# Unread products in TensorE's waits, 128-column sums of squares, and differential attention with waits by head

## The reference, cut to what matters

```python
def rmsnorm(x, g):
    y = xf * lax.rsqrt(jnp.mean(xf * xf, axis=-1, keepdims=True) + EPS)
    return (y * g.astype(jnp.float32)).astype(x.dtype)

def attend(args):                      # differential attention, a block of 128 queries
    s = jnp.einsum('bqhcd,bkhcd->bhcqk', qblk, k).astype(jnp.float32)
    s = jnp.where(mask, s, -jnp.inf)   # causal
    p = jax.nn.softmax(s, axis=-1)
    a = p[:, :, 0] - lam * p[:, :, 1]  # two maps of 64 features per head
    return jnp.einsum('bhqk,bkhe->bqhe', a.astype(v.dtype), v)
```

## Time and profile before

| | us |
|---|---|
| median of 3 runs | 3038.07 (3037.4 to 3038.97) |
| the profiled execution | 3037.71 |
| its span | 3035.9 |
| mean granted clock of TensorE | 0.951 |
| TensorE busy | 2861.8 (94%) |
| its weight loads busy | 2733.2 (90%) |
| VectorE busy | 2017.9 (66%) |
| ScalarE busy | 1543.9 (51%) |
| GpSimd busy | 593.4 (20%) |

### The profile page before, as it was taken

The page is one execution under the profiler, slowest core; times in us unless marked ns, Lnnn a source line. Parts: engine busy times, 40 slices in busy tenths (PEclk is TensorE's granted clock), DMA queues, the critical chain, the costliest instruction groups (busy, mean ns, idle before and its releaser), DMA issues.

```text
span 3035.9 us, 61036 instructions
## 1 busy us (share of the span) xinstructions
PE 2861.8 (94%) x21416; PEld 2733.2 (90%) x21416; DVE 2017.9 (66%) x4423; ACT 1543.9 (51%) x3351; POOL 593.4 (20%) x648
## 2 busy tenths in 40 slices
PE   8898989999999999899889999999998999999998
PEld 7688879999999987788889999999987899986998
DVE  6759877677677655559777666666666755555555
ACT  8452344555555544552345555555555655554554
POOL 4522680011000013114660000000033410012100
PEclk9899999999999989699999999999998989898899
DMA  4035417676676543045327655555544045441454
GB/s 153 21 120 168 123 36 227 207 233 226 204 231 217 186 135 120 27 144 178 96 70 222 188 182 185 181 186 181 186 141 125 24 143 182 152 146 35 140 182 136
DMA packets 140810, 458.19 MB, mean 151 GB/s; under 512 B 15792, under 2 KB 33584, under 8 KB 140656
## 3 DMA queue, kind: packets, MB, share of 16 engines
q1 hardware_dynamic: 135120, 436.75, 45.7%
q0 software_dynamic: 5536, 19.47, 2.2%
HBM read 446.65 MB, written 9.50 MB: 150 GB/s over the span
## 4 chain that ended last, share of the span: by engine, by line
PE 87%; DVE 5%; ACT 4%; POOL 2%; issue 1%; DMA 0%; DVEq 0%; POOLq 0%; ACTq 0%; SPq 0%
PE banks L792 64%; PE banks L949 7%; PE banks L972 3%; PE banks L1071 2%; PE banks L813 2%; POOL x_lo L2439 2%; PE banks L869 1%; ACT w_hi L503 1%; ACT arena L1422 1%; PE banks L1204 1%; PE banks L1173 1%; PE banks L1260 1%; PE banks L823 1%; DVE onehot L2031 1%; PE banks L1240 1%
## 5 line engine op out<-in xcount | busy, mean ns | idle before, releaser
L510 DVE TENSOR_TENSOR w_lo<-ring,w_hi 128x512 fp32r<-128x512 f32 x1464 | 1019.7, 703 | 723.5 <-ACT w_hi L503 716.6
L503 ACT ACTIVATE w_hi<-ring 128x512 fp32r<-128x512 f32 x1464 | 916.3, 631 | 902.1 <-PE banks L792 856.6
L792 PE MATMUL banks<-x_hi,w_hi 128*128 128x256 f32 (+1 forms) x3072 | 885.9, 288 | 36.6 <-POOL x_lo L2439 21.8
L792 PE MATMUL banks<-x_lo,w_hi 128*128 128x256 f32 (+1 forms) x3072 | 876.3, 285 | 0.0
L792 PE MATMUL banks<-x_hi,w_lo 128*128 128x256 f32 (+1 forms) x3072 | 874.0, 285 | 0.0
L792 PE MATMUL banks<-gated_hi,w_hi 128*128 128x256 f32 x2560 | 727.8, 284 | 10.0 <-DVE gated_lo L2090 9.8
L792 PE MATMUL banks<-gated_hi,w_lo 128*128 128x256 f32 x2560 | 727.3, 284 | 0.0
L792 PE MATMUL banks<-gated_lo,w_hi 128*128 128x256 f32 x2560 | 726.0, 284 | 0.0
L792 PEld LDWEIGHTS banks<-x_hi,w_hi 128*128 128x128 f32 x3072 | 588.1, 191 | 47.8 <-issue 29.3
L792 PEld LDWEIGHTS banks<-x_lo,w_hi 128*128 128x128 f32 x3072 | 588.9, 192 | 0.6
L792 PEld LDWEIGHTS banks<-x_hi,w_lo 128*128 128x128 f32 x3072 | 589.0, 192 | 0.0
(11 more groups left out here) (333 smaller groups left out, 2905.2 us busy)
## 6 DMA issues: line engine op xcount, KB each, us to landing
ring<-in_peer_v SPq DMA_DIRECT2D x256, 512.0 KB, 3.5
ring<-in_peer_u SPq DMA_DIRECT2D x192, 512.0 KB, 3.5
arena<-in_peer_u SPq DMA_DIRECT2D x64, 512.0 KB, 3.6
ring<-in_mlp_up SPq DMA_DIRECT2D x64, 512.0 KB, 3.5
ring<-in_mlp_down SPq DMA_DIRECT2D x64, 512.0 KB, 3.5
ring<-w_peer_query SPq DMA_DIRECT2D x32, 512.0 KB, 3.5
ring<-w_fox_proj SPq DMA_DIRECT2D x24, 512.0 KB, 3.5
ring<-w_nsa_proj SPq DMA_DIRECT2D x20, 512.0 KB, 3.5
```

What stands on the lines that cost most here:

```text
L503: act.activation(w_hi[:, hn % SPLITS], raw_half(hn), ACT.Copy).then_inc(hi_ready, 1)
L510: dve.tensor_tensor(w_lo[:, hn % SPLITS], raw_half(hn), w_hi[:, hn % SPLITS].bitcast(F32), ALU.subtract)\
L792: mm = pe.matmul(out, w_at(w), x, start=start and j == 0, stop=stop and j == 2, skip_group_check=True)
```

## The change

A helper `keep_warm(n)` on TensorE makes n matmuls of 128 x 128 weights and 256 columns from `gated_hi` into bank 7, and nothing reads the results. GpSimd zeroes `gated_hi` at the start, and TensorE waits for that (`gated_cleared`). The helper stands at the load (40), ahead of the waits for squares (9), for the root (6) and behind the spread (14), ahead of the differential attention (20) and behind its first three scores (6 each). `sum_chunk` takes all 128 columns of `mean_w` (whose columns are alike) and `root_of` reads the first of each 128. In the differential attention TensorE waits for the remainders head by head, ScalarE stores a unit's turned map ahead of the exponentials, and one copy takes all of its keys, since the rest of 16 keys now lies right behind the others. Also in the kernel and left as they are: `norm_twice`'s products of two columns, and all stages that aren't named here.

```diff
--- before.py
+++ after.py
@@ -88,6 +88,8 @@
 EARLY_FIRST, EARLY_BESIDE = 20, 12
 EARLY = (EARLY_FIRST + EARLY_BESIDE,) * 2
 GROUPS_OF_TWO = SEQ // 2
+WARM_LOAD, WARM_SQUARES, WARM_ROOT, WARM_SCALE = 40, 9, 6, 14
+WARM_DIFF, WARM_FILL = 20, 6
 EXPS_BEFORE = {8: 0, 16: 1}
 SECOND_FINISH, SECOND_TURN = 48, 52
 
@@ -404,7 +406,7 @@
         presum_ready, h_final, h_final_pool = sem("presum_ready"), sem("h_final"), sem("h_final_pool")
         mo_ready, mo_scaled, v_kept = sem("mo_ready"), sem("mo_scaled"), sem("v_kept")
         x_landed = [sem(f"x_landed{j}") for j in range(NC // 2)]
-        taps_landed = sem("taps_landed")
+        taps_landed, gated_cleared = sem("taps_landed"), sem("gated_cleared")
         diagonal_ready, conv_summed = sem("diagonal_ready"), sem("conv_summed")
         subkeys_landed = sem("subkeys_landed")
         early_landed = [sem(f"early_landed{j}") for j in range(4)]
@@ -807,15 +809,22 @@
                                    x_hi[:, cc_, tk_], x_lo[:, cc_, tk_], cc_ == 0, cc_ == NC - 1)
                     mm.then_inc(half_used, 1)
 
+            def keep_warm(n):
+
+                for _ in range(n):
+                    pe.matmul(banks[:, 7, 0:SEQ], gated_hi[:, 0, 0:P], gated_hi[:, 0, :], start=True, stop=True)
+
             def sum_chunk(c, tokens, start, stop):
 
                 for i, (t0, m) in enumerate(norm_tiles(tokens)):
-                    mm = pe.matmul(banks[0:m, 4, i:i + 1], squares[:, c, t0:t0 + m], mean_w[:, 0:1], start=start and i == 0,
+                    mm = pe.matmul(banks[0:m, 4, i * P:(i + 1) * P], squares[:, c, t0:t0 + m], mean_w, start=start and i == 0,
                                    stop=stop, skip_group_check=True)
                 return mm
 
             def spread_rstd(n, tokens, src=None, at=0):
 
+                if src is None:
+                    keep_warm(WARM_ROOT)
                 pe.wait_ge(rstd_ready, n)
                 src = rstd_col if src is None else src
                 for i, (t0, m) in enumerate(norm_tiles(tokens)):
@@ -826,26 +835,31 @@
 
             def sum_squares(s, tokens):
 
+                keep_warm(WARM_SQUARES)
                 for c in range(NC):
                     pe.wait_ge(squares_ready, s["sq0"] + c + 1)
                     mm = sum_chunk(c, tokens, c == 0, c == NC - 1)
                 mm.then_inc(sum_ready, 1)
                 spread_rstd(s["su0"] + 1, tokens).then_inc(rstd_spread, 1)
+                keep_warm(WARM_SCALE)
 
             def sum_presummed(s, tokens):
 
+                keep_warm(WARM_SQUARES)
                 pe.wait_ge(presum_ready, s["ps0"] + 1)
                 for c in (0, NC - 2, NC - 1):
                     pe.wait_ge(squares_ready, s["sq0"] + c + 1)
                     mm = sum_chunk(c, tokens, c == 0, c == NC - 1)
                 mm.then_inc(sum_ready, 1)
                 spread_rstd(s["su0"] + 1, tokens).then_inc(rstd_spread, 1)
+                keep_warm(WARM_SCALE)
 
             def norm(s):
                 if s.get("squares"):
                     sum_squares(s, s["tokens"])
 
             def norm_twice(s):
+                keep_warm(WARM_SQUARES)
                 for c in range(NC):
                     pe.wait_ge(squares_ready, s["sq0"] + c + 1)
                     for i, (t0, m) in enumerate(norm_tiles(SEQ)):
@@ -1232,6 +1247,8 @@
 
                 def scores(u):
                     t, hd, nk, _ = diff_unit(u)
+                    if u < HEADS:
+                        pe.wait_ge(rope_lo, NC + hd + 1)
                     if u >= 2:
                         pe.wait_ge(exp_done, u - 1)
                     for n, (q, k) in enumerate(((q_hi, dk_hi), (q_lo, dk_hi), (q_hi, dk_lo))):
@@ -1246,7 +1263,7 @@
                 def turn(u):
                     pe.wait_ge(maps_mixed, u + 1)
                     for kt, (k0, kn) in enumerate(diff_unit(u)[3]):
-                        at = kt * P if kn == P else 2 * P
+                        at = kt * P
                         mm = pe.transpose(banks[0:kn, 4 + u % 2, at:at + P], probs[:, u % 3, 0, k0:k0 + kn], ident)
                     mm.then_inc(turned, 1)
 
@@ -1256,16 +1273,18 @@
                     if u >= 2:
                         pe.wait_ge(o_kept, u - 1)
                     for kt, (k0, kn) in enumerate(keys):
-                        at = kt * P if kn == P else 2 * P
+                        at = kt * P
                         mm = pe.matmul(banks[:, 6 + u % 2, 0:P], probsT[0:kn, u % 2, at:at + P], v_tok[0:kn, kt, hd * P:(hd + 1) * P],
                                        start=kt == 0, stop=kn < P, skip_group_check=True)
                     mm.then_inc(av_done, 1)
 
+                keep_warm(WARM_DIFF)
                 pe.wait_ge(tri_rounded, 1)
-                pe.wait_ge(rope_lo, 2 * NC)
                 for u in range(n_units + 3):
                     if u < n_units:
                         scores(u)
+                    if u < 3:
+                        keep_warm(WARM_FILL)
                     if 2 <= u < n_units + 2:
                         turn(u - 2)
                     if u >= 3:
@@ -1289,6 +1308,8 @@
                 pe.wait_ge(bank_free, s["bf0"] + 16)
                 values(s["n0"] + 16, 1, D, [(META + P * i, P) for i in range(NT)])
 
+            pe.wait_ge(gated_cleared, 1)
+            keep_warm(WARM_LOAD)
             pe.wait_ge(inputs_landed, 32)
             for s in stages:
                 kind = s["kind"]
@@ -1330,9 +1351,9 @@
             def root_of(n, tokens):
 
                 act.wait_ge(sum_ready, n)
-                ins = act.activation(root_col[:, 0:NT], banks[:, 4, 0:NT], ACT.Sqrt, bias=eps)
+                ins = act.activation(root_col[:, 0:NT], banks[:, 4, 0:NT * P].rearrange("p (i n) -> p i n", n=P)[:, :, 0], ACT.Sqrt, bias=eps)
                 if tokens > SEQ:
-                    ins = act.activation(root_col[0:META, NT:NT + 1], banks[0:META, 4, NT:NT + 1], ACT.Sqrt, bias=eps[0:META])
+                    ins = act.activation(root_col[0:META, NT:NT + 1], banks[0:META, 4, NT * P:NT * P + 1], ACT.Sqrt, bias=eps[0:META])
                 ins.then_inc(root_ready, 1)
 
             def norm_twice_roots(s):
@@ -1756,12 +1777,11 @@
                     ins.then_inc(exp_done, 1)
 
                 def store(u):
-                    full = (u // HEADS + 1) * P
+                    full = len(diff_unit(u)[3]) * P
                     act.wait_ge(turned, u + 1)
                     if u >= 2:
                         act.wait_ge(av_done, u - 1)
-                    act.activation(probsT[:, u % 2, 0:full], banks[:, 4 + u % 2, 0:full], ACT.Copy)
-                    act.activation(probsT[0:META, u % 2, 2 * P:3 * P], banks[0:META, 4 + u % 2, 2 * P:3 * P], ACT.Copy)                       .then_inc(turned_stored, 1)
+                    act.activation(probsT[:, u % 2, 0:full], banks[:, 4 + u % 2, 0:full], ACT.Copy).then_inc(turned_stored, 1)
 
                 def square_sum(u):
                     t, hd = diff_unit(u)[0:2]
@@ -1771,12 +1791,12 @@
                     act.activation(square_out, o_tok[:, t, hd * P:(hd + 1) * P], ACT.Square, accum_out=sub_ss[:, u:u + 1]).then_inc(sub_squared, 1)
 
                 for u in range(n_units + 3):
+                    if 2 <= u < n_units + 2:
+                        store(u - 2)
                     if u < n_units:
                         exps(u)
                     if u == n_units:
                         load_root_table()
-                    if 2 <= u < n_units + 2:
-                        store(u - 2)
                     if u >= 3:
                         square_sum(u - 3)
                 act.wait_ge(sub_squared, n_units)
@@ -2572,6 +2592,7 @@
                     row = pair_p[:, u % 4, SEQ:2 * SEQ]
                     pool.tensor_scalar(row, row, pair_coef_[:, u % 4, 1:2], None, ALU.mult).then_inc(pair_scaled_pool, 1)
 
+            pool.memset(gated_hi[:, :, :].rearrange("p b t -> p (b t)").bitcast(F32), 0.0).then_inc(gated_cleared, 1)
             pool.memset(glu_u[:, :, 0:CONV_W - 1], 0.0)
             for s in stages:
                 kind = s["kind"]
```

## The result

The changed kernel takes 3011.33 us (median of 4 runs, 3009.87 to 3015.26) against 3038.52 us (median of 4, 3037.4 to 3039.99): the ratio is 0.9912, with a 95% interval of [0.9895, 0.9929]. It is 0.9% faster. The forecast was 2997.2, with a range of 2987 to 3017. The profiled execution took 3009.87 us, its span is 3008.0 us and TensorE's mean granted clock 0.979 (before 3037.71, 3035.9 and 0.951). By that mean the time at 0.50 went from 297 us to about 127.

The account below looks back on a forecast made before the run. TensorE, 87% of the chain that ended last, was taken as the bound, with 297 us at half clock. 3037.7 - 21 (sums of squares and spreads) - 19.5 (differential attention) = 2997.2 us, range 2987 to 3017.

Parts of the forecast that it names:

- Rival A: Differential attention: the clock falls again after the first units, leaving 1 to 2 us of gain; 3015 us, chance 0.10.
- B: Norms: idle gaps beside the unread products still let the clock fall, gain there about 8 us; 3010 us, chance 0.08.
- What bounds the kernel, and why the clock is low: Whole kernel: TensorE bounds it, 297 us at 0.50; 1-column products let the clock fall, 128 columns should hold or raise it.
- The price of a product in the sums over 272 tokens: Sums of squares: each 128-column f32 product takes 0.22 us at full clock, so 24 take 5.5 us with pipeline end.
- Its four terms: Gains at sums of load 0, layernorm 2.8, first addition to h 0.3, norm of keys and values 2.4 us.
- Sums over 256 tokens, spreads, kept projections: Sums 3.7 us each, winning 2.5 and 3.3 around the first mlp, 3.8 behind two kept projections; ten spreads win 6.0.
- Load: Sum at the load: 49 unread products end near 9 us, sums at 14.5 as before; gain 0, from -3 to +2.
- Differential attention: Units 1.75 and 2.1 us apart at full clock in place of 3.27 and 3.91; gain 19.5 us, bounds 16 to 21.
- saves only cover: Differential attention: ScalarE needs 1.5 us a unit, less than TensorE or VectorE, so one copy per unit wins no time.
- Will the clock hold: Differential attention: with TensorE near 100% busy the clock holds at 1.00, as in 20.48 us of fox attention.
- part 2: The differential attention's share of the change: gain 19.5 us; by the skill's depth-cycling rule only some 1.5 us, 3015 us.
- C: Everywhere: unread products don't hold the clock and only queue on TensorE; 33 us slower, 3071 us, chance 0.03.

Follow-up runs that it names:

- the fox runs: Changed kernel with 36 unread products in the gap ahead of fox attention: 3008.76 us; that kernel with the decay's products replaced by 128-row ones: 3000.2 us.

## Why the prediction was right or wrong

- **The number.** 27.8 of the forecast 40.6 us came. The time is inside the stated range by luck: the forecast's own range was 2987 to 3008, which ends 3 us below the measured time, and was widened to 3017 to take in rivals A and B, neither of which came true. What ate the rest stands below, and most of it is one term.
- **What bounds the kernel, and why the clock is low.** Right as far as it went: with 128 columns the sums over 256 tokens ran at 1.00, with one the clock fell within them or ahead of them. The forecast took the rows of 64 for a second reason and left it there; the fox runs bear it out, with a fall amid gapless products of which some have 16 rows.
- **The price of a product in the sums over 272 tokens: wrong, and the largest error.** The 0.22 us for a 128-column f32 product was read from weights of 128 columns and put on all three tiles. The third tile's weights have 16 columns (its 16 tokens). With 128 moving columns a chunk of three products takes 6.82/7 = 0.97 us, not 0.66. The starts of single records say where: two records of full tiles start 0.11 us apart, those of the third tile 0.12, but three of a chunk's six, at the changes between the two shapes, start 0.20 or 0.21 behind the one before. The four sums took 7.67, 6.82, 2.96 and 7.78 us for the 5.5, 4.8, 2.2 and 5.5 of the forecast, 7.2 more. Its four terms were 0, 2.8, 0.3 and 2.4, 5.5 in all, and the measured ones sum to -2.7: the difference is 8.2, the 7.2 and 0.9 at the load (below). One column for this tile gives 0.77 us a chunk, so 0.2 of the 0.3 goes with its moving columns; the last 0.1 stays with its 16-column weights, and no run takes it apart.
- **Sums over 256 tokens, spreads, kept projections.** 3.7 us each was right (3.73, 3.84), and so were 0.5 and 0.75 for a spread (5.9 of 6.0). But the two were added where they overlap. The rows under this list show the norm behind the first mlp: its squares (L1346) start when ScalarE is through with eight copies (L1614, 3.02 us) that start with the root, not with the spread. A spread that ends 0.5 us sooner leaves the next sum where it was, and the unread products ahead of it, which end about 2626.6, add 0.2. So 2.5 in place of 3.3 there, and 2.3 behind each kept projection. The unread products ahead of the short sums behind kept projections cost about what the forecast said (0.8 each for 0.7). It left them out at the last mlp, whose clock was up already: a cost and nothing to win, -1.2.
- **Load.** At -3.1 just past the bad end of its bounds (-3 to +2): 49 unread products end at 9.9, not 9, and the third tile does the rest. With 20 in their place and one column for the third tile the sums started at 6.2 and ended 4.7 and 4.8 us sooner.
- **Differential attention: right, 19.0 for 19.5.** 14.9 of it is the clock, by the run with the unread products alone. Of the other 4.2, 1.7 are closer units, which is what the edits of order are worth once the clock is up, since they are worth nothing at 0.50: 15 units of maxima in 28.89 us, 1226.67 to 1255.56, where the old order takes 30.63, and 0.6 of the 1.7 lies in the first three units. The remaining 2.4 lie behind the last maxima, where the clock was at 0.50 for 10.2 us in that run and for 3.4 in the changed kernel; that this comes from the order of the work isn't shown. Of the one copy the forecast had said that it "saves only cover"; no run has it alone at the full clock, so its part of the 1.7 isn't known.
- **Will the clock hold: right, with half a reason.** Rival A didn't come true. That fox attention held for 20 us at 1.00 was a poor witness, as its start can't hold it. And "TensorE at 100% busy didn't raise it for 47 us" isn't a law of this work: with the norms changed and no unread product in the attention it was raised after 7 us, and by the times in three executions of four; with the kernel before's norms the same attention stayed at 0.50 for 48 us. The attention's own work is the same in both. That it matters when the stage comes is argued and not shown; what decides wasn't isolated, and stays open.
- **The Trainium skill's depth-cycling of accumulation banks** ("TensorE: Matmul & The Clock Gate", section "A second HAM failure mode: psum-queue depth-cycling"), weighed against part 2, isn't seen: the attention cycles through eight banks and ran at 1.00 for 40 us. The same page of the Trainium skill, section "What's actually happening", lets the clock follow how busy TensorE has been; the fox run with the gap filled disagrees, a fall amid gapless work that the same work with 128 rows didn't have.
- **Everything else, -1.3.** The forecast allowed "a few us for where the clock's other falls lie" and put no sign on it. One new fall, at 1154.2 to 1157.6 in the values of keys and values (L1086), costs 1.6; the other stages give 0.3 back.
- **Rivals B and C.** B's place was right by accident: the norm of keys and values won nothing, but at a clock of 1.00. C is refuted at the first product behind the load.

The sum: 8.2 for the sums over 272 tokens (7.2 of it the third tile), 1.2 at the last mlp, 0.8 at the norm behind the mlp, 0.7 at the kept projections, 0.5 in the attention, 1.3 for everything else: 12.7 of the 12.8 us between 40.6 and 27.8.

Timeline of the changed kernel behind the first mlp (L815 unread products, L1614 ScalarE's copies, L1346 squares):

```profile
2622.88 3.02 ACT L1614 ACTIVATE arena<-banks,vecs 128x256 f32<-128x256 f32 x8
...
2623.70 3.00 PE L815 MATMUL banks<-gated_hi 128*128 128x256 f32 x23
...
2625.82 1.70 ACT L1346 ACTIVATE arena<-h 128x256 f32<-128x256 f32 x5
...
2626.55 1.39 PE L820 MATMUL banks<-const_a,arena 128*128 128x128 f32 x11
```

## What to carry to other kernels

Price a product by its own shape on both sides, the stationary one too, and by the change of shape between it and its neighbours. Fill the gap ahead of a long stage rather than rearranging the stage: on the kernel before, the filled gap was worth 14.4 us, the rearrangement 0 until the clock was up and 1.7 then. But measure it again when the stages ahead change: with the new norms the same unread products were worth 0.5 us by the medians, and 15 in one execution of four. Where the clock falls although TensorE has no gap, look for products of few rows or one column, and try a few wide unread ones between them (sixteen, 1.9 us of work, kept the fox attention at 1.00). Judge a piece worth 1 or 2 us by its own stage in the trace, since falls elsewhere move by up to 4 us when anything ahead of them does.

## What the runs showed of the hardware

- A product of plain f32 behind weights of 16 columns isn't cheaper than one behind 128: a chunk of two full tiles and one such takes 0.97 us with 128 moving columns and 0.77 with one, where two full tiles alone take 3.73/8 = 0.47. Records of one shape start 0.11 to 0.12 us apart, those at a change between the two shapes 0.20 to 0.21 behind the one before (128 moving columns, 1.00).
- Products of zeros that nobody reads were enough for the clock to rise: the 49 at the load start 0.21 us apart up to 7.2 us, and 0.12 apart from there.
- The granted clock fell from 1.00 to 0.50 within gapless work (TensorE busy for 3.20 of 3.20 us) that had four 16-row products of 512 columns in each pair of units. It stayed up there with 128-row ones in their place, until a stretch with idle time 5 us later, and it stayed up throughout with eight unread products of 128 rows and 256 columns among them.
- The same code in the same stage can find its clock at either level from one kernel to the next: the layernorm's sum at 5.16 and 9.12 us, the differential attention at 0.50 for 7 or for 48 us. The two kernels with the fox gap filled, the second with the decay replaced, are the same up to the fox attention; in the second alone the clock fell in the norm of keys and values (1108.2 to 1111.6), which cost 1.5 us. Executions of one kernel differ too, the ten with the edits of order by 19 us and the ten with one copy and the new order of stores by 3.3; whether filled gaps narrow this isn't shown (3.6 us over four executions).
